# Layer norms of block two read their mean and reciprocal from PSUM, and the conv taps leave the first panels

## The reference, cut to what matters

```python
def second_block(x, c, ...):
    for l in range(DEPTH):                                  # DEPTH = 2
        sh1, sc1, g1, sh2, sc2, g2 = split(silu(c) @ w_ada[l] + b_ada[l], 6)
        h = x * (1.0 + sc1) + sh1
        y = _token_mixer(h, positions, ...)                 # retention, HGRN2, 31-tap conv; gated; @ w_out
        x = _layer_norm(ALPHA * x + g1 * y, ln1_g[l], ln1_b[l])
        h = x * (1.0 + sc2) + sh2
        y = _conv_ffn(h, ...)
        x = _layer_norm(ALPHA * x + g2 * y, ln2_g[l], ln2_b[l])
    return x

def _layer_norm(x, g, b):
    mu = x.mean(-1); var = square(x - mu).mean(-1)
    return (x - mu) * rsqrt(var + LN_EPS) * g + b

# in _token_mixer: p = h @ w_in, split into rq rk rv rg gq gf gi gg ca cb gates
q = _rope(rq); k = _rope(rk) * 128 ** -0.5                  # needs cos and sin of the positions
u = _causal_dwconv(ca * sigmoid(cb), conv_w, conv_b)        # 31 taps, 512 channels
u_c = silu(_layer_norm(u, conv_ln_g, conv_ln_b))
```

## Time and profile before

| | us |
|---|---|
| median of 3 runs | 3453.51 (3451.85 to 3455.03) |
| the profiled execution, its own time | 3449.65 |
| its span, first to last instruction | 3447.8 |
| PE busy in the span | 3301.4 (96%) |
| DVE busy in the span | 2119.4 (61%) |
| ACT busy, POOL busy in the span | 1323.5 (38%), 620.4 (18%) |

### The profile page before, as it was taken

The page is one execution under the profiler, slowest core; times in us unless marked ns, Lnnn a source line. Parts: engine busy times, 40 slices in busy tenths (PEclk is TensorE's granted clock), DMA queues, the critical chain, the costliest instruction groups (busy, mean ns, idle before and its releaser), DMA issues. The chain is left out here.

```text
span 3447.8 us, 38741 instructions
## 1 busy us (share of the span) xinstructions
PE 3301.4 (96%) x15264; PEld 2645.9 (77%) x15264; DVE 2119.4 (61%) x2693; ACT 1323.5 (38%) x1716; POOL 620.4 (18%) x496
## 2 busy tenths in 40 slices
PE   8899999999999999998999998999899999989997
PEld 6577788886677788876788776888677887768886
DVE  8854566448753666457766646554677666465545
ACT  4664322234663322234332334332443332343323
POOL 2212222121212213111000232010210002320002
PEclk9999999999999999999999999999999999999999
DMA  3122455322123545231111222222222112322221
GB/s 131 42 68 79 174 196 195 122 98 67 47 71 102 195 192 191 94 115 67 68 68 68 92 93 91 94 97 97 81 79 74 61 62 92 104 74 98 98 94 65
DMA packets 72180, 344.43 MB, mean 100 GB/s; under 512 B 25152, under 2 KB 26048, under 8 KB 35648
## 3 DMA queue, kind: packets, MB, share of 16 engines
q1 hardware_dynamic: 70416, 339.12, 28.2%
q0 software_dynamic: 576, 2.33, 0.2%
q10 hardware_dynamic: 1008, 0.51, 0.1%
HBM read 340.51 MB, written 2.10 MB: 99 GB/s over the span
## 5 line engine op out<-in xcount | busy, mean ns | idle before, releaser
L897 PE MATMUL bank<-Hhi_b,whi_b 128*128 128x512 f32 x2976 | 1206.3, 405 | 68.7 <-ACT Hhi_b L2053 22.1
L898 PE MATMUL bank<-Hhi_b,wlo_b 128*128 128x512 f32 x2976 | 1165.0, 391 | 0.0
L904 PE MATMUL bank<-Hlo_b,whi_b 128*128 128x512 f32 x2976 | 1155.4, 392 | 0.9 <-DVE Hlo_b L2325 0.8
L875 DVE TENSOR_TENSOR wlo_b<-raw_b,whi_b 128x2048 fp32r<-128x2048 f32 (+2 forms) x290 | 622.5, 2147 | 480.2 <-ACT whi_b L869 479.9
L897 PEld LDWEIGHTS bank<-Hhi_b,whi_b 128*128 128x128 f32 x2976 | 562.5, 189 | 214.3 <-issue 41.6
L904 PEld LDWEIGHTS bank<-Hlo_b,whi_b 128*128 128x128 f32 x2976 | 560.2, 189 | 123.9 <-DVE Hlo_b L2325 4.9
L898 PEld LDWEIGHTS bank<-Hhi_b,wlo_b 128*128 128x128 f32 x2976 | 562.7, 189 | 119.7 <-issue 9.1
L869 ACT ACTIVATE whi_b<-raw_b 128x2048 fp32r<-128x2048 f32 (+2 forms) x290 | 511.8, 1765 | 364.8 <-PE bank L904 361.4
L897 PE MATMUL bank<-Uhi_b,whi_b 128*128 128x512 f32 x1024 | 405.6, 396 | 4.3 <-POOL Ulo_b L986 4.3
L898 PE MATMUL bank<-Uhi_b,wlo_b 128*128 128x512 f32 x1024 | 399.8, 390 | 0.0
L904 PE MATMUL bank<-Ulo_b,whi_b 128*128 128x512 f32 x1024 | 386.4, 391 | 0.0
(11 more groups left out here) (255 smaller groups left out, 3422.0 us busy)
## 6 DMA issues: line engine op xcount, KB each, us to landing
raw_b<-in_w SPq DMA_DIRECT2D x234, 1024.0 KB, 4.9
ada_b<-in_wada SPq DMA_DIRECT2D x48, 1024.0 KB, 6.9
raw_b<-in_w SPq DMA_DIRECT2D x40, 512.0 KB, 3.6
raw_b<-in_w SPq DMA_DIRECT2D x16, 768.0 KB, 4.2
rel_b<-in_rel SPq DMA_DIRECT2D x128, 24.0 KB, 2.4
X_keep<-in_x SPq DMA_DIRECT2D x4, 512.0 KB, 9.2
decay_b<-in_decay POOLq DMA_DIRECT2D x2, 1024.0 KB, 6.6
out<-X_keep SPq DMA_DIRECT2D x8, 256.0 KB, 2.0
```

The costliest lines, as they stand in the source:

```text
L875: self.nc.vector.tensor_tensor(self.wlo[n % RAW_SLOTS][:, 0:words], self.raw[n % RAW_SLOTS][:, 0:words], self.whi[n % HI_SLOTS][:, 0:words ...
L897: self.nc.tensor.matmul(out, whi[:, k, cols], xhi, start=(k == 0), stop=False)
L898: self.nc.tensor.matmul(out, wlo[:, k, cols], xhi, start=False, stop=False)
L904: mm = self.nc.tensor.matmul(out, whi[:, k, cols], xlo, start=False, stop=(k == nk - 1))
```

## The change

There are five edits, all in block two.

1. The mean is taken from columns 0 and 7 by one instruction that reads the sum in the bank `mn` (`center_column`), in place of a subtraction of the tile `msb`. `msb` is still written for POOL.
2. The reciprocal is written to a bank of its own, `rb`, and all eight columns are multiplied by it from there.
3. In layer one of the mixer no taps stand beside panels 1 and 2 (`TAPS_FIRST`).
4. The item `sines` stands behind the first piece of panel 2 instead of ahead of panel 2.
5. `taps_beside` gives no tap to a group with a reciprocal in it, and one tap to even levels instead of odd ones.

```diff
+    if "orec" in kinds:
+        return 0
     if kinds[0] == "level":
-        return group[0][4] % 2
+        return 1 - group[0][4] % 2
     return 1 if group[0][2] == "r" else 0
...
+TAPS_FIRST = (0, 0, 0)
...
-            if l == 0 and i == 2:
-                s.add("sines")
...
+                    if l == 0 and i == 2 and j == 0:
+                        s.add("sines")
                     if i <= len(heads + gates):
-                        gap(3 if kind == "z" else 2)
+                        gap(TAPS_FIRST[i] if l == 0 and i < len(TAPS_FIRST) else 3 if kind == "z" else 2)
...
         s.small.take(("ss", l, w))
+        s.small.take(("rb", l, w))
...
+    def center_column(l, w, c, *names):
+
+        nv.scalar_tensor_tensor(out=X[:, c], in0=k.out_of(("mn", l, w))[:], scalar=-1.0 / D, in1=X[:, c],
+                                op0=ALU.mult, op1=ALU.add).then_inc(*mark("dve", ("xm", l, w, c), *names))
...
-                nv.tensor_tensor(X[:, 0], X[:, 0], msb[:], ALU.subtract).then_inc(*mark("dve", ("xm", l, w, 0)))
+                center_column(l, w, 0)
                 dve.wait_ge(*after("root", l, w))
-                nv.reciprocal(buf(rs), buf(rs)).then_inc(*mark("dve", ("recip", l, w)))
+                reuse(dve, ("rb", l, w))
+                nv.reciprocal(k.out_of(("rb", l, w))[:], buf(rs)).then_inc(*mark("dve", ("recip", l, w), ("free", rs)))
...
-                    nv.tensor_tensor(X[:, c], X[:, c], msb[:], ALU.subtract).then_inc(*mark("dve", ("xm", l, w, c)))
+                    center_column(l, w, c, ("free", ("mn", l, w)))
...
-                nv.tensor_tensor(X[:, c], X[:, c], buf(("rs", l, w)), ALU.mult).then_inc(*mark("dve", *names))
+                nv.tensor_tensor(X[:, c], X[:, c], k.out_of(("rb", l, w))[:], ALU.mult).then_inc(*mark("dve", *names))
```

More of the change, by code:

```diff
@@ L2044, in act_work @@
                 act_e.activation(m2[:], mn, ACT.Square, scale=1.0 / D).then_inc(*mark("act", ("m2", l, w)))
-                act_e.activation(msb[:], mn, ACT.Copy, scale=1.0 / D).then_inc(*mark("act", ("ms", l, w), ("free", ("mn", l, w))))
+                act_e.activation(msb[:], mn, ACT.Copy, scale=1.0 / D).then_inc(*mark("act", ("ms", l, w)))
                 act.wait_ge(*after("var", l, w))
@@ L2317, in dve_work @@
                 if c == DC - 1:
-                    nv.tensor_tensor(X[:, c], X[:, c], msb[:], ALU.subtract).then_inc(*mark("dve", ("xm", l, w, c)))
+                    center_column(l, w, c, ("free", ("mn", l, w)))
                 dve.wait_ge(*after("xm", l, w, c))
-                names = [("xr", l, w, c)] + ([("free", ("rs", l, w))] if c == DC - 1 else [])
-                nv.tensor_tensor(X[:, c], X[:, c], buf(("rs", l, w)), ALU.mult).then_inc(*mark("dve", *names))
+                names = [("xr", l, w, c)] + ([("free", ("rb", l, w))] if c == DC - 1 else [])
+                nv.tensor_tensor(X[:, c], X[:, c], k.out_of(("rb", l, w))[:], ALU.mult).then_inc(*mark("dve", *names))
             elif kind == "lnlo":
```

## The result

| | before | after |
|---|---|---|
| median, beside each other on one chip | 3453.0 us (4 runs) | 3427.5 us (4 runs) |
| ratio, 95% interval | | 0.9926 (0.9909 to 0.9943) |
| the profiled execution, own time; span | 3449.65; 3447.8 | 3428.32; 3426.5 |

The change is faster by 25.5 us; forecast were 19.2 us and, for the time, 3434.3 us with a range from 3429.5 to 3442.5.

What follows compares the result with a forecast made beforehand. PE is busy nearly all of the 3447.8 us span, so only its standstill or half clock can be won; 8.8 + 1.7 - 0.4 + 3.6 + 3.1 + 2.4 = 19.2 off 3453.5 gives 3434.3 us, range 3429.5 to 3442.5.

Steps and rivals of the forecast that it cites:

- Panel 3, the clock: Start of panel 3: no fall to half clock once the long wait is gone; gain 1.7 us, from 0 to 1.75.
- the rotation: Panel 3: RQ and RK on DVE, waiting for POOL and ACT, hold `wlo` back; 5.7 us lost, 3440.0; 0.13, shared.
- banks that don't relieve DVE: Layer norms: they keep their chain despite bank operands; loss of 5.5 us, 3439.8; chance 0.08.
- a dearer bank operand: Four norms: an operand in a bank costs ten instructions a norm 0.07 us more; 2.8 us, 3437.1; chance 0.05.
- something late behind panel 3: Something, as a weight transfer or panel 4's `whi`, takes back half of panel 3's gain: 3439.5; chance 0.13, shared.
- `wlo`'s new start: Panel 3: with `whi` first on ACT and the rotation done at 1553.6, `wlo` takes 2.28; PE starts between 1555.9 and 1556.9.
- Panel 3's wait: PE between panels 2 and 3: 0.5 us of wait in place of 9.30; gain 8.8, bounds 7.5 and 9.3.
- Displaced taps: 21 taps later in DVE's queue, mostly hidden by idle time; 0.4 us lost at the first HGRN head, 0 to 0.8.
- that rival: Displaced taps are paid for: 16.4 us, 3450.7 (chance 0.05 no change), or 25 us, 3459.6 (0.04 slower).
- Six heads: Six HGRN heads: level 2 products come 0.6 us earlier without the tap behind the reciprocal; gain 3.6, bounds 1.8 and 3.9.
- Three norms: Three norms that feed a product: bank operands free DVE and POOL; 1.03 us each, 3.1 in all, bounds 0.4 and 1.4 each.
- Last norm: Last norm: eight outputs run at ACT's pace without gaps from DVE's products; gain 2.4 us, bounds 1.0 and 2.7.

Runs made afterwards that it cites:

- the first fill: Kernel before plus four idle matmuls in each of six places, missing two closing panels, some in block one and at a panel without a wait: 3448.93 against 3450.16 us (0.9994).

## Why the prediction was right or wrong

Wrong in size, right in sign and in its places. **The step that failed** is "Panel 3, the clock": it looked for half clock behind the 9.30 us wait alone (1.7 us) and had no term for any other place. In the same trace three more stretches stood in block two behind waits of 1.59, 2.12 and 1.58 us, and none of them in the first trace of after: 4.9 us (1.6, 1.7 and 1.6) that the sum lacked. Over all traces of the table it is two or three against none or one. The step also took panel 3's wait for a loss by itself. It hid the stretch behind panel 0's wait, which costs 1.6 us in the changed kernel, and only in some executions: in those without it edits 3 and 4 gain 1.6 more. The rivals on the rotation, on banks that don't relieve DVE, on a dearer bank operand and on something late behind panel 3 did not occur. The working of `wlo`'s new start came out, but not by the part that edit 4 has in it: with edit 4 undone the wait is 1.23 us. It was also wrong to lay the median 3.86 above the profiled execution as if that were a fixed offset: before's runs spread from 3445 to 3456 us.

Term by term, from the first two traces:

- Panel 3's wait: 7.95 (9.30 to 1.35), forecast 8.8, bounds 7.5 to 9.3. The text had "if each is held until POOL lets go, about 1 us more"; two of four were held.
- Its clock: 1.67. From panel 3's start to the first product it was 19.21, now 17.54 us. The window of after at that place:

```profile
1560.90:1564.40 3.50, 3.50 (x15) 2.69 (x15) 3.24 (x3) 1.07 (x1) 0.00 (x0) 1.00 0.50 211
```

- Displaced taps: the first HGRN head waits 1.38 in place of 0.70, 0.7 lost, within the 0 to 0.8 given; retention head 2 won 0.36 back (2.14 to 1.78). No panel waits longer for `wlo` because of them, so that rival falls.

```profile
1694.31 1.13 PE L2411 MATMUL bank<-RQ_b,RK_b 128*128 128x128 f32 x8 [1.38 <-DVE RQ_b L2229]
```

- Six heads: 9.3 to 5.5, 3.8 for 3.6.
- Three norms: 1.36 each and 4.1 in all, for 1.03 and 3.1. `Hlo` did end 0.54 after POOL, as reckoned. POOL was mis-sized: its subtraction takes 1.23 (7.40 for six) when not held, not the 1.29 of the earlier trace rows. The wait for `Hlo` of column 0 is gone, and the good bound of 1.4 was nearly met.
- Last norm: from PE's last wait (3429.21 before, 3410.56 after) to the end of the span 18.59, now 15.94: 2.65 for 2.4.

Together 19.8 us; with the 4.9 of the three stretches that is 24.7 of the 24.9 between these two traces. Without panel 0's stretch in the changed kernel the terms come to 21.4, of the 22.0 that the table leaves; where the other 0.6 sits is not shown.

That DVE with two tile operands and POOL hold each other up is shown by the four POOL times: 0.45 us of POOL for each such instruction, which itself takes 0.7 to 1.1 us longer (1.40 and 1.77, for 0.68 and 0.69). The GPSIMD Engine Reference of the Trainium skill (specification table) names this contention, and beside it that with DVE instructions in a 2-port perf mode. Two tile operands are not the only case here either. The angle instruction L1030 has one, and took 1.40 beside POOL; alone, in the same trace, it took 0.43 (no run shows in what mode it ran):

```profile
1544.48 0.43 DVE L1030 TENSOR_SCALAR tab_b<-tab_b 128x512 f32<-128x512 f32 x1
```

An operand in a bank cost these instructions nothing, as the source view of after shows (ns least, median, most):

```profile
L2331 DVE TENSOR_TENSOR X_keep<-X_keep,bank x32: 672/680/689, 2092.0 to 3422.5; 128x512 f32<-128x512 f32 x32
```

It is 680 ns against 685 with two tiles. The reciprocal took 3361 ns into a bank, 3340 into a tile. By an estimate from the section on the TRN2 errata in VectorE: DVE Perf Modes of the Trainium skill each product would be 65 ns longer; the measurement decides against it for these shapes.

**Open.** Why fewer stretches fall in the changed kernel. Two waits of 1.94 became 1.3, but those brought a stretch in one trace only. The other waits kept their lengths, and yet at the first closing panel of layer one the clock fell in all seven traces with before's heads and no fill, and in two of seven with edit 5 and no fill; at retention head 2 of layer two in four of seven and in none. Before's heads alone don't force it: in the trace of the first fill the waits ahead of the closing panels (1.59 and 1.58) had no fill, and the clock stayed up. TensorE: Matmul & The Clock Gate of the Trainium skill (Part 1) says that what watches PE runs freely and isn't reset by a kernel's start. That agrees with one wait bringing a fall in one execution and none in the next; it doesn't say why one kernel should have fewer, and no run here was made to tell that apart.

## What to carry to other kernels

Look at the granted clock behind short waits too, not behind the long ones only: here a wait of 1.6 to 2.1 us could cost 1.7 more, and a fill of idle matmuls in six of them bought 6 us (2 to 8 by the interval) without touching a chain. Ask of a long wait what losses ahead of it it hides: they come back when it goes. When one profile stands for a kernel, cut it at a point that both versions share and count the half-clock stretches on either side before reading a difference of a few microseconds. Where DVE instructions with two tile operands run beside GpSimd, moving one operand to a bank sped up both here.

## What the runs showed of the hardware that was not expected

The same wait, to a hundredth of a microsecond (2.12 and 2.11 us), was followed by half clock in one execution and by full clock in another. Behind waits of 1.32 to 1.52 us no trace of block two shows a fall; behind 1.58 to 2.14 it came in some and not in others. And a kernel with shorter waits can run no faster because its stretches of half clock are more (block two 1903.3 us with four, 1902.2 with one). A stretch at half clock cost nothing where PE then stood 9.3 us for another engine: with one behind panel 0 the kernel before reached panel 3's first product after 63.94 to 64.24 us, without after 63.98 and 64.16.
